# First expert layer of a transformer stack on one core: rows gathered and scatter-added by indirect DMA

## What is computed

```python
def expert_choice_ffn(h, w_router, w1, w3, w2):
    B, T, D = h.shape
    cap = max(1, EC_CAPACITY * T // N_EXPERTS)
    aff = jax.nn.softmax((h @ w_router).astype(jnp.float32), axis=-1)
    gate, idx = lax.top_k(jnp.swapaxes(aff, 1, 2), cap)
    xin = jax.vmap(lambda hb, ib: hb[ib])(h, idx)
    hid = jax.nn.silu(jnp.einsum('becd,edf->becf', xin, w1)) * jnp.einsum('becd,edf->becf', xin, w3)
    y = jnp.einsum('becf,efd->becd', hid, w2) * gate[..., None].astype(h.dtype)
    return jax.vmap(lambda yb, ib: jax.ops.segment_sum(
        yb.reshape(-1, D), ib.reshape(-1), num_segments=T))(y, idx)
```

## Time and profile before

| | us |
|---|---|
| median of 3 runs | 4849.45 |
| lowest, highest | 4847.57, 4857.23 |
| span of the profiled execution | 4855.9 |
| its own time (the only run above the span) | 4857.23 |
| TensorE busy | 4475.4 (92%) |
| VectorE, ScalarE, GpSimd busy | 1395.4, 1152.8, 524.1 |

### The profile page before, as it was taken

The page is one execution under the profiler, slowest core; times in us unless marked ns, Lnnn a source line. Parts: engine busy times, 40 slices in busy tenths (PEclk is TensorE's granted clock), DMA queues, the critical chain, the costliest instruction groups (busy, mean ns, idle before and its releaser), DMA issues. The chain is left out here.

```text
span 4855.9 us, 97813 instructions
## 1 busy us (share of the span) xinstructions
PE 4475.4 (92%) x42843; PEld 2408.1 (50%) x42843; DVE 1395.4 (29%) x3471; ACT 1152.8 (24%) x2472; POOL 524.1 (11%) x649
## 2 busy tenths in 40 slices
PE   8999999999999899997999998996888888779999
PEld 6764444444444444653434443444666666533443
DVE  1021110011001221643222225134565565532223
ACT  2142111002101221633212222033333334221111
POOL 0021000000000102101000000136222332010000
PEclk9999999999999999998999999997999999889999
DMA  3153212122222213534787774243000100039999
GB/s 138 70 175 114 69 52 74 69 85 81 73 70 89 62 52 83 164 99 171 279 292 287 284 281 170 89 136 111 23 30 30 36 30 10 13 130 409 408 406 369
DMA packets 259283, 681.36 MB, mean 140 GB/s; under 512 B 26049, under 2 KB 69105, under 8 KB 258609
## 3 DMA queue, kind: packets, MB, share of 16 engines
q1 hardware_dynamic: 234048, 608.24, 34.3%
q0 software_dynamic: 24816, 66.88, 4.7%
HBM read 645.56 MB, written 26.74 MB: 138 GB/s over the span
## 5 line engine op out<-in xcount | busy, mean ns | idle before, releaser
L2363 PE MATMUL bank<-ring,arena 128*128 128x512 f32 x2528 | 1095.1, 593 | 2.0 <-DVE arena L1804 1.6
L2363 PEld LDWEIGHTS bank<-ring,arena 128*128 128x128 f32 x2528 | 546.5, 217 | 527.0 <-issue 453.7
L2758 PE MATMUL bank<-ring,arena 128*64 128x512 f32 x2048 | 469.3, 598 | 9.9 <-DMA ring<-in_moe_w 6.2
L2363 PE MATMUL bank<-arena,ring 128*128 128x512 f32 x1024 | 442.7, 594 | 1.2 <-ACT arena L1332 0.7
L2016 DVE TENSOR_TENSOR arena<-arena,bank 128x512 f32<-128x512 f32 x280 | 174.8, 682 | 623.8 <-PE bank L2731 555.5
L2363 PEld LDWEIGHTS bank<-arena,ring 128*128 128x128 f32 x1024 | 195.2, 191 | 246.4 <-issue 244.4
L2758 PEld LDWEIGHTS bank<-ring,arena 128*64 128x64 f32 x2048 | 139.8, 136 | 310.9 <-issue 307.6
L2784 PE MATMUL bank<-ring,arena 128*64 128x512 f32 x1024 | 234.5, 604 | 2.2 <-ACT arena L1487 1.6
L2548 PE MATMUL bank<-ring,arena 128*128 128x512 f32 x512 | 219.9, 592 | 0.0
L1480 ACT ACTIVATE arena<-bank 64x512 f32<-64x512 f32 x64 | 37.7, 589 | 661.7 <-PE bank L2758 661.7
L3029 PE MATMUL bank<-arena 64*64 64x128 f32 x3840 | 161.0, 274 | 3.3 <-issue 3.3
(11 more groups left out here) (425 smaller groups left out, 5508.9 us busy)
## 6 DMA issues: line engine op xcount, KB each, us to landing
ring<-in_moe_w SPq DMA_DIRECT2D x768, 512.0 KB, 7.5
ring<-in_w_in SPq DMA_DIRECT2D x21, 2048.0 KB, 7.7
ring<-in_ada_w SPq DMA_DIRECT2D x12, 2048.0 KB, 8.1
ring<-in_ada_w SPq DMA_DIRECT2D x24, 1024.0 KB, 5.3
ring<-in_w_up SPq DMA_DIRECT2D x8, 2048.0 KB, 9.1
ring<-in_w_down SPq DMA_DIRECT2D x8, 2048.0 KB, 7.8
ring<-in_na_w_qkv SPq DMA_DIRECT2D x6, 2048.0 KB, 8.0
ring<-in_w_in SPq DMA_DIRECT2D x8, 1024.0 KB, 6.4
```

Of the source, the lines that this page charges most:

```text
L2363: ins = mm(ps[:, 0:ncol], lhs(k), rhs(k), start=(k == 0 and first), stop=(k == nk - 1))
L2758: ins = mm(ps, x_chosen[:, b, k, 0:CAP_L], w[x][:, n * W:(n + 1) * W], start=(k == 0), stop=(k == KD - 1))
```

## The change

For the first expert layer (l = 0) only:

- At the kernel's start GpSimd clears the context half of `h` and stores it three times into a new DRAM tensor `y_dram`. SP stores `xn_moe` into `x_dram` behind the first twelve weight pieces of the layer. The bf16 parts and their subtractions are not made.
- The gate products get three more columns: the affinity's three parts and the token's number (row in its tile, and the tile's offset). `route(e)` makes them two experts ahead, `gathered(e)` turns them into row numbers on DVE (one reduction, two copies, two scalings).
- GpSimd fetches the 96 chosen rows of x from `x_dram` by an indirect DMA into `x_rows` (two buffers). PE turns them (eight f32 transposes with 96 rows) in place of the gather products. ACT modulates them as before.
- y of experts 0 to 14 goes to `y_dram` by two indirect DMAs with `compute_op=ALU.add`: 128 pieces of 2 KB (latent halves) and 128 of 1 KB (context quarters). Each expert's adds wait for those of the one before. The scatter products, the turned selection and DVE's additions fall away for these experts. ACT's copy of y(e) waits for the adds of e - 2.
- After expert 14's adds GpSimd loads the sums from `y_dram` into `acc`, tile by tile, and DVE goes on as before. Expert 15 is scattered by products; its selection is turned after the hidden rows.
- Banks: the second gather half goes to bank 7, the gates to 6.

```diff
     def gather(e, half):
-        plan.add("act", "moe_gather", l, e, half, bank=(3, 1)[half])
-        if half:
-            plan.add("act", "moe_selt", l, e, width=2, bank=6)
+        plan.add("act", "moe_gather", l, e, half, bank=(3, 7 if l == 0 else 1)[half])
+        if half and l:
+            turn_selection(e)
             plan.add("dve", "moe_gates", l, e, bank=0)
+    def turn_selection(e):
+        plan.add("act", "moe_selt", l, e, width=2, bank=6)
+    def route(e):
+        if l == 0 and e < EXPERTS:
+            plan.add("dve", "moe_gates", l, e, bank=6)
+    route(0)
+    route(1)
     gather(0, 0)
     gather(0, 1)
     for e in range(EXPERTS):
         for g in range(UP_GROUPS):
-            if e >= 1 and g >= 1:
+            if l and e >= 1 and g >= 1:
                 for i, key in enumerate(scatter_keys(l)):
                     if scatter_group(l, i) == g:
                         plan.add("dve", "moe_add", l, e - 1, *key, bank=3 + i % 5)
...
                 sp.dma_start(piece(i), expert_piece(a, i)).then_inc(piece_landed[i % PIECES], 16)
+                if i == PIECES - 1:
+                    for t in range(NT):
+                        sp.wait_ge(sem("normed"), tiles_before["moe0"] + t + 1)
+                        sp.dma_start(x_dram[t * P:(t + 1) * P, :], xn_moe[:, t, :]).then_inc(sem("moe_x_stored"), 16)
...
+        nc.gpsimd.memset(h[:, LT:NT, :], 0.0).then_inc(sem("moe_zeros_set"), 1)
+        pool.wait_ge(sem("moe_zeros_set"), 1)
+        for t in range(0, NT, CT):
+            pool.dma_start(y_dram[t * P:(t + CT) * P, :].rearrange("(t p) d -> p t d", p=P), h[:, LT:NT, :]).then_inc(sem("moe_y_zeroed"), 16)
...
+            else:
+                full(pool, "turn", use, 1, KD - 1)
+                pool.wait_ge(sem("moe_x_stored"), 16 * NT)
...
+        def by_token(ap):
+            return bass.IndirectOffsetOnAxis(ap=ap, axis=0)
+        def fetch_rows(e):
+            pool.wait_ge(sem("moe_indexed"), e + 1)
+            if e >= 2:
+                full(pool, "moe_gather", 0, e - 2, 1)
+            pool.indirect_dma_start(x_rows[e % 2][0:SLOTS, :], None, x_dram, by_token(chosen_row[0:SLOTS, e % ROUTES:e % ROUTES + 1])
+                                    ).then_inc(sem(f"moe_rows_landed_{e % 2}"), 16)
+        def add_rows(e):
+            taken(pool, "moe_y", 0, e)
+            taken(pool, "moe_y_c", 0, e)
+            if e:
+                pool.wait_ge(sem("moe_rows_added"), 32 * e)
+            else:
+                pool.wait_ge(sem("moe_y_zeroed"), 16 * LT // CT + 16)
+            for ways, y, at in ((2, y_l, chosen_half), (QUARTERS, y_c, chosen_quarter)):
+                pool.indirect_dma_start(y_dram.rearrange("t (n d) -> (t n) d", n=ways), by_token(at[:, e % ROUTES:e % ROUTES + 1]),
+                                        y[:, e % 2, :], None, compute_op=ALU.add).then_inc(sem("moe_rows_added"), 16)
         experts(0)
+        fetch_rows(0)
+        fetch_rows(1)
+        for e in range(EXPERTS - 1):
+            if e + 2 < EXPERTS:
+                fetch_rows(e + 2)
+            add_rows(e)
+        pool.wait_ge(sem("moe_rows_added"), 32 * (EXPERTS - 1))
+        for t in range(NT):
+            pool.dma_start(acc[:, t, :], y_dram[t * P:(t + 1) * P, :]).then_inc(sem(f"moe_sum_landed_{t}"), 16)
...
+                    if l == 0:
+                        turn_selection(e)
                     break
                 taken(act, "moe_gates", l, e)
+                if l == 0 and e >= 2:
+                    act.wait_ge(sem("moe_rows_added"), 32 * (e - 1))
...
+                if j == 0:
+                    dve.wait_ge(sem("moe_y_zeroed"), 16 * NT // CT)
...
+            else:
+                V.memset(aff_part[:, :, :, 5], 0.0)
+                for t in range(nt):
+                    V.memset(aff_part[:, t, :, 4], float(t * P))
...
                 ps = full(dve, "moe_gates", l, e)
-                for s in range(len(streams)):
-                    ins = V.tensor_reduce(gates[:, e % 2, s:s + 1], ps[:, 4 * s:4 * s + 3], AX, ALU.add)
-                free(ins, "moe_gates", l, e)
+                if l:
+                    free(V.tensor_reduce(gates[:, e % 2, 0:1], ps[:, 0:3], AX, ALU.add), "moe_gates", l, e)
+                    return
+                b = e % ROUTES
+                if e >= ROUTES:
+                    dve.wait_ge(sem("moe_rows_added"), 32 * (e - ROUTES + 1))
+                free(V.tensor_reduce(chosen[:, b].rearrange("p s x -> p (s x)"), ps[:, 0:12].rearrange("p (g x) -> p g x", x=3), AX, ALU.add),
+                     "moe_gates", l, e)
+                taken(dve, "moe_gates", l, e)
+                lat, ctx = (chosen[:, b, s, 1:2] for s in range(2))
+                V.tensor_copy(chosen_row[0:CAP_L, b:b + 1], lat[0:CAP_L])
+                V.tensor_copy(chosen_row[CAP_L:SLOTS, b:b + 1], ctx[CAP_L:SLOTS])
+                V.tensor_scalar(chosen_half[:, b:b + 1], lat, 2.0, half_of, ALU.mult, ALU.add)
+                V.tensor_scalar(chosen_quarter[:, b:b + 1], ctx, float(QUARTERS), quarter_of, ALU.mult, ALU.add).then_inc(sem("moe_indexed"), 1)
...
+            if l == 0:
+                ins = V.tensor_copy(aff_part[:, :, :, 3], row_of.unsqueeze(2).to_broadcast([P, NT, EXPERTS]))
...
                     select(e + 2)
+                    if l == 0:
+                        gathered(e + 2)
...
+                else:
+                    dve.wait_ge(sem(f"moe_sum_landed_{t}"), 16)
                 link(V.tensor_tensor(acc[:, t, :], acc[:, t, :], moe_gate[:, int(t >= LT), :], ALU.mult))
...
                 b = e % 2
+                if l == 0:
+                    pe.wait_ge(sem(f"moe_rows_landed_{b}"), 16 * (e // 2 + 1))
+                    ps = open_("moe_gather", l, e, half).rearrange("p (k s) -> p k s", k=4)
+                    for k in range(4):
+                        d = slice((4 * half + k) * P, (4 * half + k + 1) * P)
+                        ins = turn(ps[:, k, 0:SLOTS], x_rows[b][0:SLOTS, d], ident[0:SLOTS, 0:SLOTS])
+                    close(ins, "moe_gather", l, e, half)
+                    return
                 pe.wait_ge(sem("moe_selected"), l * EXPERTS + e + 1)
                 ps = open_("moe_gather", l, e, half).rearrange("p (k s) -> p k s", k=4)
                 for k in range(4):
...
+            def route(e):
+                cols = 3 if l else 6
+                pe.wait_ge(sem("moe_selected"), l * EXPERTS + e + 1)
                 ps = open_("moe_gates", l, e)
                 if e == 0:
                     pe.wait_ge(sem("moe_aff_split"), l + 1)
-                for s, copies in enumerate((lat, ctx)):
+                for s, copies in enumerate(copies_of(e)):
                     for rows, slots, tiles in copies:
                         for t in tiles:
-                            ins = mm(ps[rows, 4 * s:4 * s + 3], sel[b][:, t, slots], aff_part[:, t, e, :], start=(t == tiles[0]), stop=(t == tiles[-1]))
+                            ins = mm(ps[rows, cols * s:cols * (s + 1)], sel[e % 2][:, t, slots], aff_part[:, t, e, 0:cols],
+                                     start=(t == tiles[0]), stop=(t == tiles[-1]))
                 close(ins, "moe_gates", l, e)
...
-            pe.wait_ge(sem("moe_part_2"), l * NT + nt)
+            if l:
+                pe.wait_ge(sem("moe_part_2"), nt)
+            else:
+                pe.wait_ge(sem("moe_ident"), 1)
+                route(0)
+                route(1)
             gather(0, 0)
             gather(0, 1)
...
                 if e + 1 < EXPERTS:
                     gather(e + 1, 1)
+                elif l == 0:
+                    turn_selection(e)
+                if l == 0 and e + 2 < EXPERTS:
+                    route(e + 2)
                 taken(pe, "moe_ht", l, e)
```

More of the change, by code:

```diff
@@ L767, in build @@
     hT_moe = n.take(KD, TOK)
+    x_rows = [Carve(n.at + b * D).take(D) for b in range(2)]
     x_part = [half_size(NT, D) for _ in range(3)]
```

90 lines of the change are left out of this document (57 added, 33 removed).

## The result

Ahead of the change the comparison gives 4853.34 us, the median of four runs from 4847.57 to 4858.48; with it 4776.45 us, the median of four runs from 4774.71 to 4784.47. The ratio is 0.9846 with an interval from 0.9832 to 0.9860: 77 us less, where 82 were forecast. Such a distance carries an interval of 6 to 11 us each way. A smaller difference between two kernels is told here from their traces, not from their times.

The account below looks back on a forecast made before the run. TensorE was taken to bound the first expert layer and the DMA engines the second. Terms -73.5, -33.0, +13, +4, +5.5, +1 and +1 sum to -82 us, from 4849.45 to 4767 us, range 4742 to 4815.

Parts of the forecast that it names:

- Scatter, -73.5: First expert layer: the scatter products, 4.90 us an expert, leave TensorE for experts 0 to 14, -73.5 us.
- Middle 3.95, -33.0: Between up and down products: 3.95 us in place of 6.15 in each of 15 experts, -33.0 us.
- Clock, +13: First down products: new idles may drop TensorE's clock, 1.7 us a fall; bounds 0 and 26 us, taken as +13.
- I take half: Clock term in the experts' middles: half of the bounds 0 to 26 us was taken, +13 us.
- Late weights, +4: DMA in the first expert layer: the adds' packets make weights come 0.3 us an expert late, +4 us.
- Prologue, +5.5: Before the first up products: the fetch chain starts them 3.5 us later, a cold first group adds about 2.
- Kernel start, +1: Clearing, estimated at 2 us, and 7.7 us of zero stores lie beside the first loads: 0 to +8, taken as +1.
- only the tail of x meets them: Kernel start: reason given for pricing the zero stores beside the first loads at only +1 us.
- End of the layer, +1: Expert 15: VectorE waits for 3.1 MB of sums loaded back, 0 to +10 us, taken as +1.
- Rival 2: First expert layer: DMA engines become the bound, period 40.0 us if adds' packets cost double, total 4801; chance 0.20.
- Rival 3: Accumulating packets hold their DMA engine for the DRAM round trip; slower than before, 4969 to over 5100 us; chance 0.15.
- rival 4: Fetches come so late that TensorE waits where it gathered; total within 10 us of before; chance 0.05.

Follow-up runs that it names:

- Experiment 5: The change with its scatter put back to products, so only the rows come by indirect load: 4833.95 us, ratio 0.9949 to the kernel before the change.
- the filled kernel: The change plus 14 and 7 dummy products in the two idles of each first-layer expert: 4747.64 us, ratio 0.9782 to the kernel before the change.
- experiment 4: The change with every add made twice and zeros stored late, 4773.84 us; again with idles filled, 4757.75; there with plain second stores 4748.11, without adds 4753.73.
- the best version: The change with hidden rows turned first, six dummy products in the remaining wait and zeros stored late: 4738.34 us, ratio 0.9743 to the kernel before the change.

## Why the prediction was right, and where its sizes were off

- *Scatter, -73.5.* Held: in this layer line 2856 runs for expert 15 alone, and up takes 21.75 us. Experiment 5 against the filled kernel holds the size.
- *Middle 3.95, -33.0.* Measured 3.88 and -34.1. The chain (SiLU, copies, hidden copy) was read rightly from rows of an order that still had the gather in it, helped by the last expert, whose 1.44 us showed the idle ahead of the hidden rows where no gather covers it. The page's idles of 0.96 and 0.41 us are the 1.05 and 0.5 of the prediction.
- *Clock, +13.* **The term that was mis-sized: +23.9**, near its bound of 26. The step that failed is "I take half": the long idle was placed between single ones, 0.71 us without a fall and 1.50 with one, as if falls came in half of the experts. They came in 15 of 16. Filling either idle leaves 7 or 11 long groups and filling both leaves none where both are filled, so both idles have a part in it. A rule that would have given 15 does not come out of these runs, since 1.44 and 0.90 us brought no fall in experiment 5.
- *Late weights, +4.* None were late. A share of 0.95 left room, and only a second set of adds (experiment 4) took it. The price of the software queue's packets was right in size: 256 x 0.147 / 16 = 2.35 us for a set of adds forecast, 1.5 to 2.2 measured. What was wrong is the 0.3 us an expert of late weights on top of it.
- *Prologue, +5.5.* 2.9 for the chain and 3.0 for the cold first group, 5.9. The issue took 1.00 us (from 2256.81), the 1.0 of the sum; from its end to the first transposes 3.7 passed, where the sum had 3.8 for landing and 0.7 behind it.
- *Kernel start, +1.* +4.5 by 2210 us, over 3 of it by 24 us: the zeros and the first weights do collide, and "only the tail of x meets them" was wrong, since TensorE waits for weights there. The clearing itself took 1.83 us, near the estimate of 2.
- *End of the layer, +1.* 0. The sums were issued at 2857.83, and no wait for them shows beside the tail of before.

The misses are +10.9, -4, +0.4, +3.5, -1 and -1.1 for the middle: +8.7 together. The two kernels' other differences gave back 3.7 and 3.9, which is chance and not foresight, and so the total came within 5 us for the distance and 9.5 for the time.

*Rivals.* Rival 2 (DMA the bound) did not occur, but a second set of adds, some 2 us of traffic an expert, brings it; the best version stands close to it. The page "DMA: Bandwidth & Descriptors" of the Trainium skill, under "Where 436 GB/s comes from", would have given a bound of 358 GB/s for the core. The window of the second layer again shows 407, and the best version runs the first layer at 378, with 13.4 MB an expert in 35.50 us: by that rule, the trace disagrees, and its 11 us did not come. Rival 3 is refuted by experiment 4, rival 4 by the table of waits.

## What to carry to other kernels

When an edit takes work off the engine that sets the pace, price what its idles will do to the clock, idles under a microsecond too, and take the upper bound when several stand close together; where an idle can't be avoided, products that nobody needs can pay (21 of them an expert gave back 25 of the 26.9 us here). Then read the chain that is left and put work of the pacing engine into its waits, and what feeds others first: the order of three small groups gave 15 us. And a doubled cost that changes no total is not yet free: look at the waits, since a second effect may have paid for it.

## What was not expected of the hardware

- Accumulating indirect stores cost the DMA engines 1.5 to 2.2 us for 384 KB in 256 rows, some 1.3 us more than plain ones, and they show more packets (2,400 more over 15 experts). The issue costs GpSimd 1.56 us for 128 rows, and 0.95 for a load of 96 rows.
- The clock fell after idles of less than a microsecond each, in more of the experts where more idle was left, and not by the idle alone: with 0.96 us left, 5 of 15 at one period and 11 of 16 at another, in a pattern that repeats over the experts; and once not after 1.44 and 0.90 us.
- One core drew 370 to 378 GB/s with the engines at a share of 1.02 to 1.04 where a part of the traffic was small packets, against 407 with weights alone.
